# A hybrid decoder layer in f32 on one core: where the row factor is multiplied into silu(gate) · up

## What is computed

```python
def rmsnorm(x, gain):
    inv = lax.rsqrt(jnp.mean(xf * xf, axis=-1, keepdims=True) + EPS)
    return xf * inv * gain
def swiglu(h, w_gate, w_up, w_down):
    return (jax.nn.silu(h @ w_gate) * (h @ w_up)) @ w_down

x = x + 0.5 * swiglu(rmsnorm(x, norm_ffn1), w1_gate, w1_up, w1_down)   # D_MODEL 2048, D_FF 5632
...
x = x + 0.5 * swiglu(rmsnorm(x, norm_ffn2), w2_gate, w2_up, w2_down)
```

## Time and profile before

| | |
|---|---|
| median of 3 runs | 1699.76 us (1699.75 to 1700.0) |
| the profiled execution | 1699.39 us |
| its span, first to last instruction | 1697.6 us |
| TensorE busy | 1686.7 us, 99% |
| VectorE busy | 1341.0 us, 79% |
| ScalarE busy | 886.4 us, 52% |
| GpSimd busy | 233.5 us, 14% |
| mean DMA rate | 214 GB/s |
| one superblock of the loop | 41.48 us (the silu at 174.82 to the one at 216.30) |

### The profile page before, as it was taken

The page is one execution under the profiler, slowest core; times in us unless marked ns, Lnnn a source line. Parts: engine busy times, 40 slices in busy tenths (PEclk is TensorE's granted clock), DMA queues, the critical chain, the costliest instruction groups (busy, mean ns, idle before and its releaser), DMA issues.

```text
span 1697.6 us, 21641 instructions
## 1 busy us (share of the span) xinstructions
PE 1686.7 (99%) x7554; PEld 1399.4 (82%) x7554; DVE 1341.0 (79%) x1585; ACT 886.4 (52%) x1049; POOL 233.5 (14%) x397
## 2 busy tenths in 40 slices
PE   9999999999999999999999999999999999999998
PEld 7788888888888888888888888888888888888886
DVE  7999999999956566587977889999999999654554
ACT  6655555555544444454554556555555555443443
POOL 0222222222220000000040002222222222200000
PEclk9999999999999999999999999999999999999999
DMA  7677777777685555665545566777777777955552
GB/s 275 213 231 226 223 222 224 229 233 230 218 309 189 191 195 198 210 202 192 171 150 173 186 236 183 232 230 226 229 233 227 222 223 222 333 198 189 188 195 99
DMA packets 194107, 362.95 MB, mean 214 GB/s; under 512 B 12232, under 2 KB 24448, under 8 KB 193664
## 3 DMA queue, kind: packets, MB, share of 16 engines
q1 hardware_dynamic: 175136, 336.70, 59.4%
q0 software_dynamic: 16976, 24.14, 6.4%
q10 hardware_dynamic: 1936, 1.32, 0.3%
HBM read 346.39 MB, written 4.19 MB: 207 GB/s over the span
## 4 chain that ended last, share of the span: by engine, by line
PE 98%; DVE 1%; ACT 0%; issue 0%; DMA 0%; SPq 0%; ACTq 0%; DVEq 0%
PE banks L533 25%; PE banks L535 25%; PE banks L534 25%; PE banks L626 6%; PE banks L628 6%; PE banks L627 6%; PE banks L519 2%; PE banks L552 1%; PE banks L522 1%; PE banks L735 0%; PE banks L759 0%; DMA raw<-in_w_gate 0%; PE banks L747 0%; DVE w_lo L1199 0%; PE banks L613 0%
## 5 line engine op out<-in xcount | busy, mean ns | idle before, releaser
L1199 DVE TENSOR_TENSOR w_lo<-raw,w_hi 128x1024 fp32r<-128x1024 f32 x302 | 371.4, 1234 | 267.5 <-ACT w_hi L881 266.2
L1010 ACT ACTIVATE w_hi<-raw 128x1024 fp32r<-128x1024 f32 (+1 forms) x440 | 425.0, 997 | 288.7 <-PE banks L535 182.8
L1423 DVE TENSOR_TENSOR w_lo<-raw,w_hi 128x1024 fp32r<-128x1024 f32 (+1 forms) x440 | 492.1, 1146 | 52.2 <-ACT w_hi L1010 51.3
L881 ACT ACTIVATE w_hi<-raw 128x1024 fp32r<-128x1024 f32 x302 | 318.5, 1059 | 411.3 <-PE banks L535 385.5
L533 PE MATMUL banks<-w_hi,act 128*128 128x512 f32 x1056 | 411.6, 390 | 0.0
L535 PE MATMUL banks<-w_lo,act 128*128 128x512 f32 x1056 | 410.9, 389 | 0.0
L534 PE MATMUL banks<-w_hi,act 128*128 128x512 f32 x1056 | 410.8, 389 | 0.0
L533 PE MATMUL banks<-w_hi,h 128*128 128x512 f32 x832 | 323.8, 389 | 0.0
L535 PE MATMUL banks<-w_lo,h 128*128 128x512 f32 x832 | 323.7, 389 | 0.0
L534 PE MATMUL banks<-w_hi,h 128*128 128x512 f32 x832 | 323.7, 389 | 0.0
L1835 POOL DMA_DIRECT2D turned<-squared x320 | 170.8, 558 | 681.6 <-DVE squared L1274 675.9
(11 more groups left out here) (170 smaller groups left out, 1260.7 us busy)
## 6 DMA issues: line engine op xcount, KB each, us to landing
raw<-in_w_down SPq DMA_DIRECT2D x88, 1024.0 KB, 5.0
raw<-in_w_gate SPq DMA_DIRECT2D x84, 1024.0 KB, 5.2
raw<-in_w_up SPq DMA_DIRECT2D x84, 1024.0 KB, 5.5
raw<-in_w_in SPq DMA_DIRECT2D x32, 1024.0 KB, 5.4
raw<-in_w_out SPq DMA_DIRECT2D x16, 1024.0 KB, 5.0
turned<-squared POOLq DMA_DIRECT2D x320, 32.0 KB, 1.8
raw<-in_w_up POOLq DMA_DIRECT2D x20, 512.0 KB, 7.1
raw<-in_w_up SPq DMA_DIRECT2D x8, 512.0 KB, 9.2
```

What stands on the lines that cost most here:

```text
L881: act_e.activation(w_hi[:, s, :], raw[:, (p // 2) % RAW_SLOTS, off:off + PIECE], ACT.Copy).then_inc(hi_ready, 1)
L1010: act_e.activation(fast_split(w_hi, p, shift), fast_raw(name, shift), ACT.Copy).then_inc(hi_ready, 1)
L1199: dve.tensor_tensor(w_lo[:, s, :], raw[:, (p // 2) % RAW_SLOTS, off:off + PIECE], w_hi[:, s, :].bitcast(F32), ALU.subtract).then_inc(lo_re ...
L1423: dve.tensor_tensor(fast_split(w_lo, p, shift), fast_raw(ORDER[p], shift), fast_split(w_hi, p, shift).bitcast(F32), ALU.subtract).then_inc ...
```

## The change

The factor `r_col` is no longer applied by VectorE with the product, but by ScalarE right behind silu. A new semaphore `gate_ready` is raised by silu; ScalarE waits for it itself, multiplies the two halves of `gu` by `r_col` in place with two activations of 512 columns (Copy with a scale), and only then raises `silu_ready`. VectorE's product becomes one `tensor_tensor` of 1024 columns.

```diff
@@ silu, after the first superblock @@
                     ins = act_e.activation(gu[:, t, :], banks[:, GATE_BANK + t, :], ACT.Silu,
                                            scale=r_col[:, t:t + 1])
+                ins.then_inc(gate_ready, 1)
+                scale_gate(f["sb"])
+
+            def scale_gate(n):
+
+                act_e.wait_ge(gate_ready, n + 1)
+                for t in range(2):
+                    ins = act_e.activation(gu[:, t, :], gu[:, t, :], ACT.Copy,
+                                           scale=r_col[:, t:t + 1])
                 ins.then_inc(silu_ready, 1)
@@ silu_fast, after each of the other superblocks @@
-            def silu_fast(merges):
+            def silu_fast(n, merges):
 
                 act_e.wait_ge(folded, merges + 1)
                 for t in range(2):
                     ins = act_e.activation(gu[:, t, :], gu[:, t, :], ACT.Silu,
                                            scale=r_col[:, t:t + 1])
-                ins.then_inc(silu_ready, 1)
+                ins.then_inc(gate_ready, 1)
+                scale_gate(n)
@@ merged_product @@
                 dve.wait_ge(merged, merges)
                 dve.wait_ge(silu_ready, n + 1)
-                for t in range(2):
-                    ins = dve.scalar_tensor_tensor(gu[:, t, :], folds[:, t, :], r_col[:, t:t + 1],
-                                                   gu[:, t, :], ALU.mult, ALU.mult)
-                ins.then_inc(product_ready, 1)
+                dve.tensor_tensor(gu[:, :, :], folds[:, :, :], gu[:, :, :],
+                                  ALU.mult).then_inc(product_ready, 1)
```

More of the change, by code:

```diff
@@ L260, in layer_kernel @@
         act_ready = sem("act_ready")
+        gate_ready = sem("gate_ready")
         silu_ready = sem("silu_ready")
@@ L1037, in fast_gate_up @@
                         round_h(fi - 1, SB * i - SB, turned)
-                silu_fast(merges_of(f, i))
+                silu_fast(fi, merges_of(f, i))
             def down(f):
```

## The result

The changed kernel takes 1702.78 us in the median (1702.29 to 1703.63, 19 runs), the kernel before 1699.78 (1699.63 to 1702.69, 19 runs). The ratio is 1.0017 (95% interval 1.001 to 1.0024): **3.0 us slower**, where 3.7 was forecast.

The account below looks back on a forecast made before the run. TensorE, busy 99%, was taken to bound the kernel; losses of 1.6 and 0.4 us in the loop, 1.4 and 0.25 behind the half steps' first superblocks sum to 3.7, giving 1703.5 us (range 1701.0 to 1706.5).

Parts of the forecast that it names:

- TensorE's room at the end of a superblock: Before TensorE's first weight load of F0: 1.21 us of delay allowed in 18 of the loop's 20 superblocks, less in two.
- The cost on ScalarE: Behind silu: F0's rounding 1.40 us later, from lost overlap 0.10, wait on itself 0.06 and the pair 1.24.
- The lateness and what is caught up: At F0's load in the loop: 0.19 us late, 0.10 caught up by the fourth load, 0.09 lost each time.
- behind the first superblock: First half step, where TensorE waits already: F0's load at 56.70 instead of 55.28, 1.4 us lost.
- in the second half step: Behind its first superblock: F0's load at 1035.76 against 1035.41, late 0.35, 0.25 us lost.
- the loop and the two places ahead of `down`: 18 superblocks of the loop at 0.09 us lost each, 1.6 us, plus 0.4 us for two with less room.
- The two superblocks with a late silu: In the loop, room taken as 1.08 and 1.12 us: late by 0.32 and 0.28, 0.22 and 0.18 lost, 0.4 us.
- VectorE's saving: At VectorE's product: 0.19 us less, 22 times, ahead of idle stretches, so given nothing in the sum.
- The first (no short stalls): Rival: with a free wait on itself the loop's load is 0.03 late, all caught up; 1701.3 us; chance 0.22.
- The second (the delay doesn't die out): Rival: VectorE's delay or a late T3 makes the next superblock's silu later, in 20 places; 1707 to 1708 us; chance 0.19.
- The third: Rival: VectorE's saving reaches silu and moves it forward, at best 4.2 us, 1695.6 us; chance 0.03.
- The fourth: Rival: Copy and Silu not in one table, so a table load behind each silu; chance 0.01.

Follow-up runs that it names:

- experiment 1: Changed kernel with the scaling pair moved behind the rounding of G10 (in `down`, of its third piece), TensorE waiting for gate_ready: 1699.71 us.
- experiment 2: Changed kernel with gate_ready raised by each of the two silus, each scaling waiting for its own silu only: 1701.65 us.
- experiment 3: Changed kernel with VectorE's two old scalar_tensor_tensor put back, the row factor applied twice: 1703.15 us.
- experiment 4: Kernel before with VectorE's product as one operation of 1024 columns, ScalarE unchanged, the row factor left out: 1699.98 us.
- experiment 6: Changed kernel with one more scaling activation of 512 columns behind the pair: 1717.29 us.
- experiment 7: Silu table loaded earlier, folds cleared earlier: with the scaling behind G10's rounding 1700.88 us, with the changed kernel 1702.95; clearing still earlier, 1703.10 and 1705.50.

## Why the prediction came out as it did

**The mechanism was right, at each step that carries the sum.** TensorE's room at the end of a superblock, not ScalarE's 52% or VectorE's 79%, decided it. Shown by experiment 1: the same work a few microseconds later costs nothing.

**The cost on ScalarE.** Forecast 1.40 (0.10 + 0.06 + 1.24), measured 1.37. The wait on itself costs 0.03 and the lost overlap of 0.10; I had taken 0.06 between 0.04 and 0.08. The price by a wait that costs nothing (1.24) stood beside it, with the Trainium skill, "VectorE: DVE Perf Modes", section "The DRAIN you can't avoid"; so far as the signals go the runs agree: experiment 2 has one behind each silu and its delay is 1.23. What costs is the wait for the instruction just ahead: with it the delay is 1.37, so it is worth 0.14 on ScalarE. (The 0.7 us more on ScalarE and 0.7 less on VectorE in the prediction's first paragraph are not what its working uses: the pair is 1.34 us more, and VectorE saves 0.19.)

**The lateness and what is caught up.** Forecast 0.19 late, 0.10 caught up; measured 0.15 and 0.11. Experiment 2 adds that the 0.10 is not a room that is free up to its edge: with the load 0.01 late, 0.01 to 0.04 a place is lost without a wait in the view. What the prediction left out is that TensorE, once disturbed, falls behind by a further 0.01 to 0.04 over the next dozen loads; in the changed kernel too, which is why 0.15 late and 0.11 caught up make 0.047 at some places and 0.080 at others.

**The terms of the sum**, forecast and measured: behind the first superblock 1.4 and 1.45; in the second half step 0.25 and 0.21; the loop and the two places ahead of `down` 2.0 and 1.40. The last is the term that was mis-sized. In the 16 plain places of the loop 0.06 is lost in the mean where I had 0.09, which makes 0.45 of the difference: the wait on itself is 0.03 and not 0.06, so the load comes 0.15 and not 0.19 late. The two superblocks with a late silu, for which I had 0.4, make 0.28: in the changed kernel's trace they don't stand out and lose 0.047 and 0.080 like the rest. They were no property of the place. In the kernel before, ScalarE waited in both for a chunk of `w_up` that landed late, 1.42 and 0.91 us; this is the first:

```profile
127.05 3.07 ACT L1010 ACTIVATE w_hi<-raw 128x1024 fp32r<-128x1024 f32 x3 [1.42 <-DMA raw<-in_w_up]
```

Against that, the two places ahead of `down` lost 0.15 each and not 0.09, since the load starts 0.06 later behind its rest there.

**VectorE's saving was worth nothing**, as forecast: experiments 3 and 4 from both sides. VectorE had more to spare than the 0.33 of the prediction, which had not counted the idle 0.34 between the two stretches: 0.69 of its idle time is still there ahead of the folds.

**The rivals.** The first (no short stalls) gave 1701.3; with the wait on itself taken away, the kernel took 1701.65, so its price was about right; its condition, a wait on itself that is free, was not met, and its rule that a load late by 0.03 loses nothing isn't true either. The second (the delay doesn't die out) is refuted by the changed kernel and by experiment 3, without VectorE's saving: in both, silu starts 4.82 ahead of where F0's load would be in step, and 4.81 in the kernel before. Experiment 6 could not have shown it growing, since TensorE's own stall takes up what is added. The third fell with experiment 4. The fourth needed a table load behind silu; there is none, both traces have nine in all.

**The chances.** The bound of 0.2% lay in the middle of my sum's own range, so 0.53 for slower and 0.44 for the same was the toss of a coin, and on which side the time fell was luck: it is "the same" by 0.4 us (3.0 against 3.4).

## What to carry to other kernels

Where one engine is at 99%, ask of an added instruction not how long it is but what stands behind it in its engine's program, and how much room that has: here 1.34 us of work, done 22 times, was free at one place and cost 3 us a few rows earlier. Read the room at every place where the work is added, the first pass of a loop apart: one place without room made half of the loss, the 21 with room the rest. And once the room is used up, the next 0.6 us cost 0.6 us each time.

## What was not expected of the hardware

**VectorE and GpSimd in each other's way, with an edge.** The traces of all four kernels with the earlier table load show 1.24 lost at 889 us, where GpSimd works on the pooling windows while VectorE makes rests. With the late scaling alone (experiment 1), VectorE's rest of the mixing weights comes first, and GpSimd's next instruction behind it takes 2.49:

```profile
882.14 1.22 DVE L1764 TENSOR_TENSOR mix_lo<-pool_w_sb,mix_hi 128x1024 fp32r<-128x1024 f32 x1 [1.38 <-ACT mix_hi L1160]
883.28 1.63 DVE L1212 TENSOR_TENSOR w_lo<-raw,w_hi 128x1024 fp32r<-128x1024 f32 x1
...
882.22 2.49 POOL L1836 TENSOR_SCALAR window<-window 128x512 f32<-128x512 f32 x1
```

With the table loaded early as well, ScalarE's rounding of these weights starts 0.27 later behind TensorE's scores, VectorE's rest comes 0.20 behind GpSimd's instruction instead of 0.08 ahead of it, and the order is turned round: GpSimd takes 1.49 and VectorE pays, most at the next rest, which starts 0.04 behind GpSimd's next instruction.

```profile
882.50 1.50 DVE L1772 TENSOR_TENSOR mix_lo<-pool_w_sb,mix_hi 128x1024 fp32r<-128x1024 f32 x1 [1.65 <-ACT mix_hi L1169]
883.92 2.34 DVE L1221 TENSOR_TENSOR w_lo<-raw,w_hi 128x1024 fp32r<-128x1024 f32 x1
...
882.30 1.49 POOL L1844 TENSOR_SCALAR window<-window 128x512 f32<-128x512 f32 x1
883.88 1.30 POOL L1845 TENSOR_TENSOR u<-window,u 128x512 f32<-128x512 f32 x1
```

So the same VectorE form of 1.22 took 1.63 or 2.34 here, and TensorE then waits for an attention head. Beside each other the rows show that the two delay each other by up to 1.1 us, and that 0.3 us of difference in a start turns round who pays. The Trainium skill, "SBUF — State Buffer", section "Who interferes with whom", has a mechanism: a VectorE instruction with two inputs in SBUF contends with a GpSimd instruction that reads SBUF, since its second input comes through a read port that both share, and the shared pair of ports is an exclusive lock. If the first one holds it to its end, two of the rows agree: GpSimd's at 882.22 comes 0.08 behind VectorE's, which runs 1.14 longer, and takes 2.49 instead of 1.49; VectorE's at 883.92 comes 0.04 behind a GpSimd instruction of 1.30 and takes 1.12 longer. Two don't: at 882.50 VectorE starts 0.20 behind an instruction of 1.49 and takes only 0.28 longer, and at 883.28 it takes 0.41 longer beside one that ends 1.43 later. Why ScalarE started 0.27 later in the second case is open.

**The start scatters.** The first 15 us, which load x and the first weights, differ by up to 0.9 between the traces; from there on a superblock repeats to some hundredths, unless a chunk lands late (experiment 7). That is why differences of 0.2 us could be read from matmuls laid side by side, and not from medians.
